# GpSimd raises mean plus epsilon to the power -0.5 in the grouped norm of y, in place of VectorE's reciprocal and ScalarE's square root

## The reference: what is computed

```python
y = y.reshape(b, L, D_INNER) * jax.nn.silu(z.astype(f32))
yg = y.reshape(b, L, SSM_GROUPS, D_INNER // SSM_GROUPS)      # 8 groups of 512 channels
yg = yg * lax.rsqrt(jnp.mean(yg * yg, axis=-1, keepdims=True) + EPS)
y = (yg.reshape(b, L, D_INNER) * ssm_norm.astype(f32)).astype(x.dtype)
branch_a = y @ w_ssm_out
```

## Time and profile before

| | |
|---|---|
| median of 3 runs | 2870.84 us (2868.09 to 2876.43) |
| profiled execution, its own time | 2867.64 us |
| span of the profiled execution (first to last instruction) | 2865.8 us |
| granted TensorE clock, mean over the span | 0.995 of full speed |
| busy: PE, DVE, ACT, POOL | 98%, 62%, 41%, 11% |
| norms of y (lines 1387, 1389, 1005, 1393) | 8, of which 7 in the loop |
| one iteration of the loop | about 116.3 us |

### The profile page before, as it was taken

How to read it: one execution, slowest core, us unless ns; L and a number is a source line. 1 busy time by engine, 2 the same in 40 slices (tenths; PEclk the granted TensorE clock), 3 DMA queues, 4 the chain that set the end, 5 groups by cost and what they waited for, 6 DMA issues and landing times.

```text
span 2865.8 us, 53271 instructions
## 1 busy us (share of the span) xinstructions
PE 2816.3 (98%) x19312; PEld 2757.7 (96%) x19312; DVE 1780.4 (62%) x2250; ACT 1166.3 (41%) x1729; POOL 325.3 (11%) x456
## 2 busy tenths in 40 slices
PE   8899999999999999999999999999999999999998
PEld 7799999999999899999999999999999999999998
DVE  7777877778778655555455555655555555555564
ACT  4454444544545333333333335433333333333453
POOL 2222222222223100000000001000000000000100
PEclk9999999999999999999999999999999999999999
DMA  8788686886877565555555555455545555555463
GB/s 219 180 211 204 173 221 169 207 215 162 222 184 192 162 175 160 154 146 147 148 146 149 152 151 159 136 154 151 148 146 151 153 148 148 146 146 152 141 178 111
DMA packets 893378, 474.15 MB, mean 165 GB/s; under 512 B 154089, under 2 KB 886689, under 8 KB 892977
## 3 DMA queue, kind: packets, MB, share of 16 engines
q1 hardware_dynamic: 819097, 431.02, 55.4%
q10 hardware_dynamic: 73528, 39.39, 4.8%
q0 software_dynamic: 672, 2.66, 0.2%
HBM read 447.50 MB, written 25.47 MB: 165 GB/s over the span
## 4 chain that ended last, share of the span: by engine, by line
PE 85%; DVE 7%; DMA 3%; issue 3%; ACT 1%; SPq 1%; POOL 0%; ACTq 0%; DVEq 0%; POOLq 0%
PE ps L1710 27%; PE ps L1711 27%; PE ps L1712 27%; DMA raw<-in_w_ssm_out 2%; DVE wlo L1083 2%; DVE cv L1204 1%; SPq L599 1%; PE ps L2099 1%; DVE var L1389 1%; PE ps L1858 1%; PE ps L1859 1%; PE ps L1868 0%; PE ps L1816 0%; PE ps L1953 0%; PE ps L1970 0%
## 5 line engine op out<-in xcount | busy, mean ns | idle before, releaser
L1710 PE MATMUL ps<-n_hi,whi 128*128 128x320 f32 x4144 | 1286.8, 311 | 0.8 <-DVE chunk L1452 0.6
L1712 PE MATMUL ps<-n_hi,wlo 128*128 128x320 f32 x4144 | 1281.4, 309 | 0.0
L1711 PE MATMUL ps<-n_lo,whi 128*128 128x320 f32 x4144 | 1281.4, 309 | 0.0
L1083 DVE TENSOR_TENSOR wlo<-raw,whi 128x1024 fp32r<-128x1024 f32 x746 | 926.0, 1251 | 480.4 <-ACT whi L720 479.4
L720 ACT ACTIVATE whi<-raw 128x1024 fp32r<-128x1024 f32 x746 | 784.3, 1057 | 842.3 <-PE ps L1712 762.2
L1710 PEld LDWEIGHTS ps<-n_hi,whi 128*128 128x128 f32 x4144 | 779.0, 188 | 7.2 <-issue 3.7
L1711 PEld LDWEIGHTS ps<-n_lo,whi 128*128 128x128 f32 x4144 | 779.1, 188 | 1.4
L1712 PEld LDWEIGHTS ps<-n_hi,wlo 128*128 128x128 f32 x4144 | 778.7, 188 | 0.0
L1710 PE MATMUL ps<-c_hi,whi 128*128 128x320 f32 x1728 | 537.7, 311 | 13.0 <-DVE b_stack L1350 10.1
L1711 PE MATMUL ps<-c_lo,whi 128*128 128x320 f32 x1728 | 535.1, 310 | 0.0
L1712 PE MATMUL ps<-c_hi,wlo 128*128 128x320 f32 x1728 | 535.1, 310 | 0.0
(11 more groups left out here) (299 smaller groups left out, 1791.9 us busy)
## 6 DMA issues: line engine op xcount, KB each, us to landing
raw<-in_w_in SPq DMA_DIRECT2D x322, 512.0 KB, 4.5
raw<-in_w_ffn_gate SPq DMA_DIRECT2D x88, 512.0 KB, 4.6
raw<-in_w_ffn_up SPq DMA_DIRECT2D x88, 512.0 KB, 5.0
raw<-in_w_ffn_down SPq DMA_DIRECT2D x88, 512.0 KB, 4.3
raw<-in_w_ssm_out SPq DMA_DIRECT2D x64, 512.0 KB, 4.9
hq<-in_state_ssm SPq DMA_DIRECT2D x512, 32.0 KB, 3.1
hs<-in_state_ssm ACTq DMA_DIRECT2D x32, 512.0 KB, 5.2
out_ssm_sample<-hs ACTq DMA_DIRECT2D x32, 512.0 KB, 3.7
```

Of the source, the lines that this page charges most:

```text
L1083: tt(wlo[slot][:], raw[slot][:], whi[slot][:].bitcast(F32), SUB).then_inc(lo_split, 1)
L1710: mm(out, w_h, x_h, start=first, stop=False)
L1711: mm(out, w_h, x_l, start=False, stop=False)
L1712: return mm(out, w_l, x_h, start=False, stop=last)
```

## The change

GpSimd gets a function `root(g)`: it waits for DVE's `vsum_read` and raises `var` in place to the power -0.5, with `tensor_tensor` whose second operand is one column that holds -0.5, broadcast over the 320 columns. It signals `yrstd`, for which DVE waits as before. DVE's reciprocal with its wait, and ACT's wait and square root, go. In the loop `root` stands at the step `norm`, behind GpSimd's work for unit x 1; for the last group it stands first in GpSimd's work for unit c 0 of `sc`. The column with -0.5 is a spare one of `c_own_mem`, written once at the start.

```diff
@@ allocation
         gnrm, gd = c_own_mem[:, 2 * P:2 * P + 4], c_own_mem[:, 2 * P + 4:2 * P + 8]
+        minus_half = c_own_mem[:, 2 * P + 8:2 * P + 9]
@@ ACT
                 elif kind == "norm":
-                    act.wait_ge(vinv, g)
-                    activate(rstd[:], var[:], ACT.Sqrt).then_inc(yrstd, 1)
                     if seg.name == "sc":
                         ssm_over(act)
@@ DVE
                     dve.wait_ge(vs_done, g)
                     ts(var[:], ps[:, VS_BANK, 0:NT], GROUPS / DI, EPS, MUL, ADD).then_inc(vsum_read, 1)
-                    dve.wait_ge(vsum_read, g)
-                    v.reciprocal(var[:], var[:]).then_inc(vinv, 1)
                     dve.wait_ge(yrstd, g)
@@ GpSimd
+            def root(g):
+                pool.wait_ge(vsum_read, g)
+                g_.tensor_tensor(var[:], var[:], minus_half.broadcast_to([P, NT]), ALU.pow).then_inc(yrstd, 1)
+
             def tasks(seg, it, step):
                 kind, j = step[0], step[-1]
                 g = it if seg.name in ("prologue", "ssm") else GROUPS
+                if kind == "norm" and seg.name == "ssm":
+                    root(g)
...
-                            g_.memset(c_own_mem[:], 0.0)
+                            g_.memset(c_own_mem[:, 0:2 * P], 0.0)
+                            g_.memset(minus_half, -0.5)
...
                 elif kind == "unit" and step[1] == "c":
                     if seg.start == 0 and j == 0:
+                        root(GROUPS)
                         ssm_over(pool)
```

## The result

The changed kernel takes 3245.3 us (median of 4 runs, 3244.09 to 3247.45) against 2870.11 us before (median of 4 runs as well): a ratio of 1.130, with a 95% interval of 1.128 to 1.132. That is 375 us more. The prediction was slower by 69 us, within 2860 to 3110 us. The direction was right, and the size was off by more than a factor of five.

What follows compares the result with a forecast made beforehand. The prediction took PE to bound the kernel, with DVE's norm on the path through PE's waits for `b_stack`. Seven loop norms at 8.5 us plus 9.5 us behind the last gave +69 us: 2940 us, range 2860 to 3110.

Steps and rivals of the forecast that it cites:

- What bounds the kernel: DVE's norm makes `b_stack` late for PE, without slack in the loop; 2.73 us from `var` to `chunk` can be replaced.
- The price of the pow: One 128x320 pow on GpSimd at each norm: 25 to 30 steps, 7 to 20 us, taken as 12 us.
- far end: Upper end for one pow on GpSimd, each step waiting for the one before: 25 x 0.27 x 4.5 = 31 us.
- The dearer estimate: Pow on GpSimd at 4 cycles per element and step, 25 steps at 1.2 GHz: 27 us, total about +200 us.
- Hand-overs: Signals DVE to GpSimd and back at each norm: 0.16 and 0.09 us, together 0.25 us.
- What a longer norm costs: DVE 9.5 us later at each norm; PE's wait for `b_stack` grows by that less 1.5 us (0 to 2.2) absorbed.
- The half clock: PE restarting at 1.2 GHz after each loop stall: 0.5 us lost, of 0 to 1.5, partly hidden in waiting for `b_stack`.
- the prediction's sum: Seven loop norms at 8.5 us, 59.5 us, plus 9.5 us behind the last norm: +69 us.
- ScalarE's table loads: At each norm: the root's load (1.28 us) worth nothing; the reload precedes `c_hi`, for which DVE waits 0.99 us.
- A pow worked almost value by value: Rival: one pow on GpSimd above 31 us; with 60 us, +453 us and 3324 us; chance 0.13.
- The quick pow: Rival: one pow on GpSimd of 0.88 us, DVE 1.6 us earlier at each norm, -12 us, 2859 us; chance 0.10.
- the one wait in `sc`: PE's 2.4 us wait for `c_lo` behind the last norm, followed by 2.9 us at half speed, 1.5 us lost.

Runs made afterwards that it cites:

- a pow of 4.5 us: The changed kernel with the pow on only 26 of the 320 columns: 2885.1 us, 1.0045 of the kernel before.
- one of 0.87 us: The changed kernel with the pow on only 3 of the 320 columns: 2854.9 us, 0.9952 of the kernel before.
- the probe: The kernel before with pows of several shapes, exponents and values, and a product, on a scratch tile behind GpSimd's last work; only their records count, product 0.72 us.
- 12.3 us: The changed kernel with the pow on only 75 of the 320 columns: 2932.9 us, 1.0215 of the kernel before.
- 160: The changed kernel with the pow on only 160 of the 320 columns, pow 25.83 us: 3039.7 us, 1.0587 of the kernel before.
- either half of the change: The kernel before without VectorE's reciprocal, 2864.4 us (0.9972), or without ScalarE's square root, 2863.5 us (0.9973).
- the two kernels with late loads: The kernel before with ScalarE's `hs` loads issued behind `lows`, 2856.2 us (0.9959); the same with the root taken first from PSUM, 2864.6 us (0.9984).

## Why the prediction was wrong

**What bounds the kernel.** Right. The norm was on the path in the loop: a pow of 4.5 us cost 15 us and one of 0.87 us gave 15. Only "with no slack at all" was too strong, since PE's waits grew by less than the delay.

**The price of the pow: this step failed.** It said "25 x 0.27 = 7 us to 30 x 0.68 = 20 us" and took 12; measured are 51.3. A column costs 159 ns. At the step's own rate, a memset's 0.27 us for 320 columns, that is 190 steps and not 25. The count came from VectorE's hand-written series, which says how much arithmetic a logarithm is and not how GpSimd works out a power. The "far end" of 31 us, a factor of 4.5 borrowed from VectorE's reciprocal, was no bound at all: it went into the range as one, and the time fell outside.

**The dearer estimate.** The estimate from the Trainium skill (GPSIMD Engine Reference, on performance pitfalls: 27 us, +200 us) was nearer than the sum's 12 us, but still half of what was measured. The "~2× slower" that the Trainium skill gives for elementwise work with two inputs (GPSIMD Engine Reference, on engine selection) is somewhat more than the product of the probe shows, 0.72 us against 0.51 us for VectorE's step, and says nothing of a pow, 71 times as long as the product.

**Hand-overs.** 0.25 us assumed, 0.11 measured.

**What a longer norm costs.** At 12.3 us the kernel lost 63 us where the sum said 69. The split was off in a way that cancels, which is luck. The prediction had 1.5 us of each delay given back, 2.2 at most, and 0.5 us lost to the clock, 1.5 at most. Measured, the norm is 9.7 us longer and PE's waits grow by 6.4 us at each, so 3.3 us are given back; with 160 and 320 columns it is 3.3 and 3.2 us. The weight load behind the norm takes 3.4 to 4.1 us at 75 columns, where 4.9 was reckoned. The half clock is paid in full: "PE restarts before `b_stack` is there, so a part of it is hidden" is wrong, since PE no longer waits for `b_stack` at all. It costs 2.2 us at each norm at 12.3 us and 2.1 at 51.3, of which 0.4 was there before. For 51.3 us the prediction's sum gives 48.9 - 1.0 = 47.9 us in the loop, 7 x 47.9 + 48.9 = 384 us, against 375 measured.

**ScalarE's table loads.** The load in front of the root was called "worth nothing", and the reload was given a part of 0.99 us. The prediction followed one chain, though, where a second of nearly the same length ran through ScalarE, with the reload (1.28 us) on it; that one ends last once VectorE's is shorter. What the table loads are worth by themselves no run shows: without the root PE's waits shrink by the root's own 4 us. For the result it did not matter.

**The rivals.** "A pow worked almost value by value" was given 0.13 and came nearest: 3324 us for 60 us. Its reason, a routine that branches on its argument, has nothing for it in the records, which are equal for every value and exponent tried. The quick pow would have given -15 us and not -12, since half clock cost 3.2 us before and not the 1.5 us of the one wait in `sc`.

## What to carry to other kernels

An operation whose price stands in no row should be probed by itself, in a corner of a kernel where its engine idles, before anything is built on it; a range made of analogies from other engines is not a bound. When the sum is right except for one term, dialling that term (here the number of columns) shows both in four runs; the waits and the clock must then be read one by one, for a sum can come out right with two parts wrong. And before shortening the chain that ends last, look for the second one beside it: here either half of the change gave 6 or 7 us, both together 15. Moving three DMA issues gave 12 us without touching the norm, but it shortened both chains at once, ScalarE's and that of the weight load.

## What the runs showed of the hardware that was not expected

- GpSimd's pow takes 0.39 us and 0.159 us for each column of fp32, from 1 to 320 columns. At 320 columns it is the same on 1, 16, 64 and 128 partitions, and at 80 columns for exponents -1, -0.5, 0.5, 1 and 2. A product of 320 columns takes 0.72 us, an addition 0.88.
- After stalls of 8 us PE ran 3.0 to 5.2 us at a granted clock of 0.50, after stalls of some 48 us 3.5 to 4.6 us, which costs about 2 us each time. After six waits of 2.1 to 4.6 us (26 columns) it was 3.3 to 5.0 us.
- A DMA issue on ScalarE's queue can hold the engine: the third of three loads of 512 KB took 1.8 to 4.2 us to issue in the two kernels with late loads, where the first took 0.4.
- The weight load behind the norm took 6.3 to 8.7 us in the kernel before, where ScalarE begins its loads of `hs` (512 KB each) ahead of it, and 3.4 to 3.7 us where it issues them behind it.
